# One-hot gate products placed one token at a time inside the second expert pass of a two-block transformer kernel

## The chip, the cores and the metric

The kernel runs on one core of one Trainium2 chip. The metric is the device time of one execution in microseconds (us); lower is better.

## The reference, cut to what matters

Two transformer blocks follow each other on 256 tokens of width 1024. The change lies in the last part of the second block, a feed-forward layer that picks 128 of 16,384 experts for each token:

```python
# PEER_HEADS 8, PEER_TOPK 16, PEER_NKEYS 128: e = i1 * 128 + i2, for each token 8 * 16 picks
e = (i1 * PEER_NKEYS + i2).reshape(TOK_BLOCK, PEER_HEADS * K)
gate = jax.nn.softmax(best_s, axis=-1).reshape(TOK_BLOCK, PEER_HEADS * K)
u = expert_u[e]
act = jax.nn.gelu(jnp.einsum('td,ted->te', xb, u), approximate=False)
coef = (gate * act.astype(jnp.float32)).astype(xb.dtype)
return jnp.einsum('te,ted->td', coef, expert_v[e])
```

## The kernel before, in words

The kernel gathers nothing: it computes all 16,384 experts, as 128 tiles of 128 (a tile `e` holds the experts of one second key with all 128 first keys), and zeroes what was not picked. Each weight tile is 128 x 1024 in fp32 and passes through three buffers (`ring`, RING = 3). Since a matmul in fp32r keeps only the high part of a number, ScalarE copies each tile to `w_hi` (`split_high`, L474), and VectorE (two tiles of three) or GpSimd (the third) forms `w_lo` = tile - `w_hi` (`split_low`, L488). The DMA of a tile (L528) waits until the tile three before it was split.

**First expert pass.** TensorE multiplies the tiles of `expert_u` with the tokens (`expert_up`, L673) and ScalarE puts gelu of it into `act_all`, 128 experts x (128 tiles x 256 tokens). **Second expert pass.** For each tile of `expert_v` (`expert_down`, L1130) TensorE adds coefficient times weights into the PSUM banks 4 to 7, which hold 256 tokens x 1024 outputs: 12 matmuls with 512 columns, six for each half of the tokens (three products high x high, high x low, low x high, two column halves each). The coefficients of tile e are split just ahead: ScalarE writes `h_hi` (`high_coef`, L2045) and VectorE `h_lo` (`low_coef`, L1709), into two sets of buffers (e % 2).

**Gates.** The mask with the softmax weights is made by matmuls with one-hot operands, for 64 tiles (half of the second keys) at a time. For four tokens (a "quad" q) VectorE writes the one-hot rows of the first key (`first_keys(q)`, L1656, 128 x 512, three buffers in turn, semaphore `hot_1_ready`). For eight tokens (a group g = q // 2) it writes those of the second key (`second_keys(g)`, L1667), and GpSimd multiplies them by the softmax weights (`weigh(g)`, L625, `hot_2_ready`). TensorE forms one 128 x 64 product for each token into a bank of its own (`four_gates(q)`, L1095, banks 0 to 2 in turn, fp32), and VectorE multiplies the bank into `act_all` (`gated_acts(g)`, L1677, `gates_used`). Quads 0 to 63 serve the first half of the tiles, quads 64 to 127 the second half, which the second pass needs only from tile 64 on. So quads 68 to 127 are computed during the second pass.

**The order of work around the change** is written out by hand for each engine, and each engine executes its list in order. In the loop of 60 steps (tiles k = 2 to 61):

- TensorE: `expert_down(k)`, which waits for `w_lo` of tile k and for `coef_low` k + 1, then `four_gates(66 + k)`.
- VectorE, step k (`down_dve`, L1720): `low_coef(k + 2)`, which waits for ScalarE's `high_coef(k + 2)`; `split_low` of tile k + 3, where it is not GpSimd's; `first_keys(67 + k)`; then `gated_acts(33 + k // 2)` for odd k, `second_keys(34 + k // 2)` for even k.
- ScalarE, step k: `high_coef(k + 2)`, which waits until TensorE has signalled the end of tile k, since that frees the `h` buffers; then `split_high` of tile k + 3.
- GpSimd, step k: `split_low` of every third tile, and for even k `weigh(34 + k // 2)`.

Two lists side by side, of the same step:

```python
# VectorE                                  # TensorE
second(k, i, GB)                           expert_down(k, i, GB)
if k < 61:                                 four_gates(66 + k, i)
    first_keys(67 + k, i)
```

Of the kernel before, what the change touches and what calls it, by code (L numbers as in the profile page):

```python
# [122 lines left out]
def bass_transformer_pair(nc, x_t, meta_t, kept, first, second, rel, w1_in, w1_cmp, w1_out, w1_ffn,  # L123
# [3 lines left out]
    with ExitStack() as ctx:  # L127
# [3 lines left out]
        def sem(name):  # L131
            return ctx.enter_context(nc.semaphore(name))
# [15 lines left out]
        psum = ctx.enter_context(nc.psum_tensor("psum", [P, 8, 512], F32))  # L148
# [75 lines left out]
        coef_low = sem("coef_low")  # L224
        tiles_used = sem("tiles_used")
# [121 lines left out]
        GB = 12  # L347
# [10 lines left out]
        hot_2 = lambda g: hot_2_sets[g % 2]  # L358
        hot_1_read = lambda q: hot_1(q) if q % 3 == 0 else hot_1(q).bitcast(F32)
        gate_bank = lambda g: 6 + g % 2 if g < GROUPS else g % 3  # L360
# [76 lines left out]
        hot_1_ready = sem("hot_1_ready")  # L437
        hot_2_raw = sem("hot_2_raw")
        hot_2_ready = sem("hot_2_ready")
        gates_done = sem("gates_done")  # L440
        gates_used = sem("gates_used")
# [14 lines left out]
        base, n = [], 0  # L456
# [6 lines left out]
        def trip(v, i=None, per=BODY):  # L463

            return v if i is None else i * per + v
# [10 lines left out]
        def low_wait(eng, n, i=None, per=BODY):  # L476

            if n % RING == 2:
                eng.wait_ge(low_ready2, trip(n // RING + 1, i, per // RING))
            else:  # L480
                eng.wait_ge(low_ready, trip(n // RING * 2 + n % RING + 1, i, per // RING * 2))
# [9 lines left out]
        def tile_split(pe, n, i=None, per=BODY):  # L491

            low_wait(pe, n, i, per)
            return n % RING
# [3 lines left out]
        B_V = B_EXP + NE  # L498
# [158 lines left out]
        def _(pe):  # L657
# [25 lines left out]
            def down(slot, par):  # L683

                for m in range(KD):
                    for w, h in ((w_hi, h_hi), (w_hi, h_lo), (w_lo, h_hi)):
# [9 lines left out]
                      start=True, stop=True).then_inc(brow_sum, 1)  # L696
# [3 lines left out]
            with pe.Fori(0, Z1 // BODY) as i:  # L700
                for k in range(BODY):
                    slot = tile_split(pe, B_IN1 + k, i)
# [4 lines left out]
            for qt in range(2):  # L707
                for k in range(KD):
                    mm = pe.matmul(psum[:, 6, qt * 24:(qt + 1) * 24], sq[:, k, qt * P:(qt + 1) * P],
                                   colv("gates", k * 24, (k + 1) * 24), start=(k == 0), stop=(k == KD - 1))  # L710
# [4 lines left out]
            for kv in range(2):  # L715
                for j in range(4):
                    slot = tile_split(pe, B_CMP + kv * 4 + j)
                    for r in range(4):
                        for n, (w, x) in enumerate(((w_hi, x_hi), (w_hi, x_lo), (w_lo, x_hi))):
                            mm = pe.matmul(psum[0:2 * N_CMP, kv, 0:2 * P], x[:, 4 * kv + j, r * 2 * N_CMP:(r + 1) * 2 * N_CMP],  # L720
                                           w[:, slot, 2 * r * P:2 * (r + 1) * P],
                                           start=(j + r + n == 0), stop=(j + r + n == 8))
                    mm.then_inc(tiles_used, 1)

            for b, zt in enumerate((ZVS, ZVW)):
                for kt in range(2):
                    mm = pe.transpose(psum[:, 4, (b * 2 + kt) * P:(b * 2 + kt + 1) * P],
                                      z1[:, zt, kt * P:(kt + 1) * P], const("ident"))
            mm.then_inc(vtok_sum, 1)
            pe.wait_ge(cmp_hid_ready, 2)  # L730
            for kv in range(2):
                for c in range(2):
                    mm = pe.transpose(psum[:, 2, (2 * kv + c) * 32:(2 * kv + c) * 32 + 2 * N_CMP],
                                      cmp_act[0:2 * N_CMP, kv, c * P:(c + 1) * P], const("ident")[0:2 * N_CMP, 0:2 * N_CMP])
            mm.then_inc(cmp_hid_sum, 1)
            pe.wait_ge(cmp_hid_ready, 3)
            for c in range(2):
                pe.matmul(psum[:, 5, 0:2 * N_CMP], colv("w2k", c * P, (c + 1) * P), cmp_hid[:, 0, c, :],
                          start=(c == 0), stop=(c == 1))
            for g in range(N_KV):  # L740
                for c in range(2):
                    mm = pe.matmul(psum[0:N_CMP, 5, 64 + g * HD:64 + (g + 1) * HD],
                                   cmp_hid[:, 1, c, g * N_CMP:(g + 1) * N_CMP], colv("w2v", c * HD, (c + 1) * HD),
                                   start=(c == 0), stop=(c == 1))
# [7 lines left out]
            for n in range(6):  # L752
                pe.matmul(psum[:, BIAS_BANKS[n], :], const("flip"), bias_up.rearrange("p h k -> p (h k)")[:, n * 512:(n + 1) * 512],
                          start=True, stop=True).then_inc(bias_turned, 1)
# [66 lines left out]
            for m in range(KD):  # L821
                slot = tile_split(pe, B_OUT1 + m)
# [63 lines left out]
            for n, (lo, hi, w, src) in enumerate(((0, HD, "wa_up", 20), (HD, P, "wa_up", 20), (0, P, "g_up", 21))):  # L886
                pe.wait_ge(lowrank_ready, 2)
                for m in range(4):
                    if n == 2:
                        pe.wait_ge(up_ready, m + 1)  # L890
                    mm = pe.matmul(psum[:, (4 * n + m) % 8, 0:T2], colv(w, m * P, (m + 1) * P)[lo:hi], z2[lo:hi, src, 1:T2 + 1],
                                   start=True, stop=True)
                    mm.then_inc(up_sum, 1)

            for r, (ready, src) in enumerate(((kk_squares, sq4), (bonus_in, sq4))):
# [3 lines left out]
                for m in range(4):  # L899
                    mm = pe.matmul(psum[:, 4 + m, 0:T2], const("headones"), src[:, m, :], start=True, stop=True)  # L900
# [6 lines left out]
            def fm(x, h, t0, nt):  # L907

                q = slice(h % 2 * HD, (h % 2 + 1) * HD)
                return x[q, h // 2, t0:t0 + nt]  # L910

            for tg in range(3):
# [3 lines left out]
                for n, src in enumerate((alpha, z2[:, 16:20, 1:T2 + 1], kappa_end, beta_end)):  # L916
                    if tg == 0 and n == 2:
                        pe.wait_ge(kappa_ready, 1)
                    for m in range(4):
                        mm = pe.transpose(psum[0:nt, n, m * P:(m + 1) * P], src[:, m, t0:t0 + nt], const("ident"))  # L920
                    mm.then_inc(tm_sum, 1)
                for hh in range(2):
# [14 lines left out]
                    for n, kinds in enumerate((((beta, alpha), (kappa, alpha)), ((alpha, beta),), ((beta, rho), (kappa, rho)))):  # L937
                        for odd in range(2):
                            for k, (x, y) in enumerate(kinds):
                                for h in (odd, odd + 2):  # L940
                                    mm = pe.matmul(out(2 * n + odd, 2 * k + h // 2), fm(x, 4 * hh + h, t0, nt),
                                                   fm(y, 4 * hh + h, t0, nt), start=True, stop=True)
# [38 lines left out]
                    for h in range(4):  # L981
                        q = slice(h % 2 * HD, (h % 2 + 1) * HD)
# [3 lines left out]
                        mm = pe.matmul(psum[q, 5, c:c + nt], yh(h, HD, P), G(G_QT, h), start=False, stop=True)  # L986
                    mm.then_inc(eo_sum, 1)
                    if tg < 2:
                        for p in range(2):
                            n = 2 * u + p  # L990
                            pe.wait_ge(spread_b, 3 * u + 2 + p)
                            pe.wait_ge(spread_y, 3 * u + 1 + 2 * p)
                            for x in range(2):
                                h = 2 * p + x
                                q = slice(x * HD, (x + 1) * HD)
# [5 lines left out]
                                mm = pe.matmul(psum[q, b0 + 1, :], tmh(3, h), ex(2), start=False, stop=True)  # L1001
# [6 lines left out]
                for c in range(nt // CH):  # L1008
                    slot = 8 if tg and c == 0 else c
                    pe.wait_ge(state_ready, 8 * tg + c + 1)  # L1010
                    if tg < 2:
                        for h in range(8):
                            q = slice(h % 2 * HD, (h % 2 + 1) * HD)
                            mm = pe.matmul(psum[q, c % 2, h // 2 * HD:(h // 2 + 1) * HD], f_t[q, h // 2, c, :],
                                           state[q, h // 2, slot, :], start=True, stop=True)
                        mm.then_inc(rec_sum, 1)
                    for h in range(8):
                        q = slice(h % 2 * HD, (h % 2 + 1) * HD)
                        mm = pe.matmul(psum[q, 2, h // 2 * P + c * CH:h // 2 * P + (c + 1) * CH], state[q, h // 2, slot, :],
                                       e_t[q, h // 2, c * CH:(c + 1) * CH], start=True, stop=True)  # L1020
# [24 lines left out]
            for m in range(KD):  # L1045
                if m >= 4:
                    pe.wait_ge(merged_ready, m - 3)
                slot = tile_split(pe, B_MID + 16 + m)
# [3 lines left out]
            for m in range(KD):  # L1052
                slot = tile_split(pe, B_OUT2 + m)
# [4 lines left out]
            for m in range(16):  # L1058
                slot = tile_split(pe, B_Q + m)
# [3 lines left out]
            for n in range(2):  # L1063
                slot = tile_split(pe, B_SUB + n)
                if n == 0:
                    pe.wait_ge(q_copied, 16)
                for qt in range(2):
                    if n == 1:
                        pe.wait_ge(score_copied, 2 * qt + 2)
                    for k in range(8):  # L1070
                        for p, w in enumerate((w_hi, w_lo)):
                            mm = pe.matmul(psum[:, 4 * qt + k // 4 + 0, (k % 4) * P:(k % 4 + 1) * P],
                                           query[:, 8 * n + k, qt * P:(qt + 1) * P], w[:, slot, k * P:(k + 1) * P].bitcast(F32),
                                           start=(p == 0), stop=(p == 1))
# [6 lines left out]
            def expert_up(e, i=None, per=BODY):  # L1081
                slot = tile_split(pe, B_EXP + e, i, per)
                pe.wait_ge(expert_act, trip(e + 1, i, per))
                project(slot, psum[:, e % BODY, 0:TX], TX).then_inc(tiles_used, 1)

            def four_gates(q, i=None):

                g = q // 2
                pe.wait_ge(hot_1_ready, trip(q + 1, i, GB))
                if q % 2 == 0:  # L1090
                    pe.wait_ge(hot_2_ready, trip(g + 1, i, GB // 2))
                    pe.wait_ge(gates_used, trip(g + 1, i, GB // 2))
                bank = psum[:, gate_bank(g), :].rearrange("p (e t) -> p t e", t=8)
                for t in range(4):
                    mm = pe.matmul(bank[:, 4 * (q % 2) + t, :], hot_1_read(q)[:, t, :], hot_2(g)[:, 4 * (q % 2) + t, :],  # L1095
                                   start=True, stop=True)
                mm.then_inc(gates_done, 1)

            pieces(B_EXP, E0 - 1, pe, expert_up)

# [2 lines left out]
            for n in range(3):  # L1103
                for qt in range(2):
                    mm = pe.transpose(psum[:, 6 + n // 2, (n % 2) * TX + qt * P:(n % 2) * TX + (qt + 1) * P],
                                      chosen[:, n, qt].rearrange("p a b -> p (a b)"), const("ident"))
# [9 lines left out]
            for q in range(60, 64):  # L1116
                four_gates(q)
# [6 lines left out]
                    pe.matmul(psum[:, 4 + 2 * tt + k // 4, (k % 4) * P:(k % 4 + 1) * P], hx1[:, k, tt * P:(tt + 1) * P],  # L1124
                              const("ident"), start=(k % 4 == 0), stop=False, is_transpose=True, skip_group_check=True)

            def half_down(slot, par, tt):
                for w, h in ((w_hi, h_hi), (w_lo, h_hi), (w_hi, h_lo)):
                    for half in range(2):
                        mm = pe.matmul(psum[:, 4 + 2 * tt + half, :], h[:, par, tt * P:(tt + 1) * P],  # L1130
                                       w[:, slot, half * 512:(half + 1) * 512], start=False, stop=False,
                                       skip_group_check=True)
                return mm

            def expert_down(e, i=None, per=BODY):
                slot = tile_split(pe, B_V + e, i, per)
                pe.wait_ge(coef_low, trip(e + 1, i, per))
                half_down(slot, e % 2, 0)
                half_down(slot, e % 2, 1).then_inc(tiles_used, 1)

            expert_down(0)
            expert_down(1)
            for q in range(64, 68):
                four_gates(q)
            with pe.Fori(0, 5) as i:
                for k in range(2, 2 + GB):
                    expert_down(k, i, GB)
                    four_gates(66 + k, i)
            pieces(B_V, NE - 2 - 62, pe, lambda k, i: expert_down(62 + k, i))
            expert_down(NE - 2)  # L1150
            slot = tile_split(pe, B_V + NE - 1)
# [1009 lines left out]
```

## Time and profile before

| what | value |
|---|---|
| median of 3 runs (lowest, highest) | 1799.74 us (1796.98, 1811.25) |
| profiled execution, its own time | 1801.02 us |
| profiled execution, span of its trace | 1799.2 us |
| TensorE matmuls busy | 1625.5 us, 90% of the span |
| VectorE busy | 1123.3 us, 62% |
| ScalarE busy | 773.6 us, 43% |
| GpSimd busy | 473.7 us, 26% |
| mean granted clock of TensorE | 0.949 of full speed |

The profile is one execution. Its span runs from the first to the last instruction; what lies around it is 1.8 us. Engines are named PE (TensorE matmuls), PEld (its weight loads), DVE (VectorE), ACT (ScalarE), POOL (GpSimd), SP (the engine that issues the DMAs). Matmuls are pipelined and their ends are modelled, so a busy PE is not PE at its peak. A row with x2 joins two instructions, and its duration is from the start of the first to the end of the last.

### The profile page before, as it was taken

How to read it: one execution, taken by the hardware profiler on the slowest of the kernel's cores; microseconds unless marked ns; L12 is line 12 of the kernel's file. 1: busy time of each engine (PE TensorE's matmuls, PEld its weight loads, DVE VectorE, ACT ScalarE, POOL GpSimd, SP SyncE). 2: the span in 40 equal slices, each digit the busy share in tenths (PEclk: the TensorE clock that was granted, in tenths of full speed). 3: DMA queues.
4: the chain of work that ended last, by engine and by line, in shares of the span. 5: the costliest groups of instructions: out<-in, count | busy, mean ns of one | idle time of the engine just before them, and what ended most of it. 6: DMA issues, size and time to landing. Idle time of an engine off the chain costs nothing.

```text
span 1799.2 us, 32624 instructions
## 1 busy us (share of the span) xinstructions
PE 1625.5 (90%) x11880; PEld 1478.1 (82%) x11880; DVE 1123.3 (62%) x1793; ACT 773.6 (43%) x1203; POOL 473.7 (26%) x235
## 2 busy tenths in 40 slices
PE   6988789997994777788899999999999999999998
PEld 5965689996993665578899999999998888888886
DVE  3366366565358566675428898656667777775554
ACT  3455455554443111124446566544332333335554
POOL 1210112221231221012222323433333333332322
PEclk8997899999997899789999999999998999999999
DMA  6540235553451000014445555544442444446654
GB/s 217 187 133 1 94 106 185 186 176 117 131 167 54 1 2 1 2 60 151 133 150 177 172 187 175 164 141 146 144 140 94 141 139 135 136 139 198 187 196 154
DMA packets 66240, 234.70 MB, mean 130 GB/s; under 512 B 8216, under 2 KB 9256, under 8 KB 66176
## 3 DMA queue, kind: packets, MB, share of 16 engines
q1 hardware_dynamic: 65776, 232.25, 39.8%
q0 software_dynamic: 400, 1.59, 0.2%
q8 instruction: 42, 0.69, 0.2%
q14 instruction: 22, 0.18, 0.0%
HBM read 232.74 MB, written 1.06 MB: 130 GB/s over the span
## 4 chain that ended last, share of the span: by engine, by line
PE 57%; issue 30%; DVE 7%; POOL 3%; ACT 2%; DMA 0%; SPq 0%; POOLq 0%; DVEq 0%; ACTq 0%
PE psum L673 25%; PE psum L1130 18%; PE psum L1095 6%; PE psum L687 3%; POOL w_lo L488 3%; PE psum L949 2%; DVE big L1387 1%; DVE w_lo L488 1%; DVE big L1401 1%; ACT w_hi L474 1%; PE psum L661 1%; DVE big L1428 0%; DMA big<-rel 0%; DVE x_hi L1656 0%; DVE big L1456 0%
## 5 line engine op out<-in xcount | busy, mean ns | idle before, releaser
L673 PE MATMUL psum<-x_hi,w_hi 128*128 128x256 f32 (+1 forms) x2192 | 628.9, 287 | 44.3 <-DVE x_lo L1193 23.3
L673 PE MATMUL psum<-x_lo,w_hi 128*128 128x256 f32 (+1 forms) x2192 | 623.4, 284 | 0.0
L673 PE MATMUL psum<-x_hi,w_lo 128*128 128x256 f32 (+1 forms) x2192 | 623.0, 284 | 0.0
L488 POOL TENSOR_TENSOR w_lo<-ring,w_hi 128x1024 fp32r<-128x1024 f32 x144 | 363.7, 2526 | 939.9 <-ACT w_hi L474 939.9
L488 DVE TENSOR_TENSOR w_lo<-ring,w_hi 128x1024 fp32r<-128x1024 f32 x290 | 366.1, 1263 | 247.1 <-ACT w_hi L474 246.4
L474 ACT ACTIVATE w_hi<-ring 128x1024 fp32r<-128x1024 f32 x434 | 456.1, 1051 | 86.0 <-PE psum L673 47.7
L673 PEld LDWEIGHTS psum<-x_hi,w_hi 128*128 128x128 f32 x2192 | 420.4, 192 | 50.5 <-issue 31.3
L673 PEld LDWEIGHTS psum<-x_hi,w_lo 128*128 128x128 f32 x2192 | 420.4, 192 | 0.0
L673 PEld LDWEIGHTS psum<-x_lo,w_hi 128*128 128x128 f32 x2192 | 418.4, 191 | 0.0
L1130 PE MATMUL psum<-w_hi,h_hi 128*128 128x512 f32 x512 | 164.4, 402 | 0.0
L2045 ACT ACTIVATE h_hi<-big 128x256 fp32r (+1 forms) x128 | 53.3, 417 | 250.6 <-PE psum L1130 243.1
L1130 PE MATMUL psum<-w_lo,h_hi 128*128 128x512 f32 x512 | 159.3, 393 | 0.0
L1130 PE MATMUL psum<-w_hi,h_lo 128*128 128x512 f32 x512 | 158.2, 390 | 0.0
L1709 DVE TENSOR_TENSOR h_lo<-big,h_hi 128x256 fp32r<-128x256 f32 x128 | 75.3, 589 | 117.9 <-ACT h_hi L2045 117.5
L2018 ACT ACTIVATE big<-psum 128x256 f32 (+1 forms) x128 | 49.0, 383 | 201.1 <-PE psum L673 200.9
L1130 PEld LDWEIGHTS psum<-w_hi,h_lo 128*128 128x128 f32 x512 | 96.4, 188 | 21.4
L1130 PEld LDWEIGHTS psum<-w_lo,h_hi 128*128 128x128 f32 x512 | 96.4, 188 | 21.1
L1130 PEld LDWEIGHTS psum<-w_hi,h_hi 128*128 128x128 f32 x512 | 92.0, 190 | 15.5
L1327 DVE SCALAR_TENSOR_TENSOR big<-psum,big 128x255 f32<-128x255 f32 x88 | 42.4, 482 | 71.0 <-ACT big L1868 69.5
L949 PE MATMUL psum<-big 128*128 128x128 f32 (+4 forms) x480 | 64.3, 299 | 19.4 <-DVE big L1456 7.7
L949 PEld LDWEIGHTS psum<-big 128*128 128x128 f32 (+1 forms) x480 | 55.5, 183 | 27.5 <-DVE big L1456 8.7
L625 POOL TENSOR_TENSOR kept_sb<-kept_sb,sq 128x512 f32<-128x512 f32 x32 | 35.9, 1122 | 108.1 <-DVE kept_sb L1667 108.1
(297 smaller groups left out, 2004.2 us busy)
## 6 DMA issues: line engine op xcount, KB each, us to landing
ring<-experts SPq DMA_DIRECT2D x256, 512.0 KB, 3.3
ring<-w_ffn SPq DMA_DIRECT2D x66, 512.0 KB, 3.4
ring<-w_in SPq DMA_DIRECT2D x46, 512.0 KB, 3.6
ring<-w_mid SPq DMA_DIRECT2D x24, 512.0 KB, 3.3
ring<-w_out SPq DMA_DIRECT2D x16, 512.0 KB, 4.0
ring<-w_q SPq DMA_DIRECT2D x16, 512.0 KB, 3.6
ring<-w_cmp SPq DMA_DIRECT2D x8, 512.0 KB, 3.3
big<-bias_rows POOLq DMA_DIRECT2D x1, 1536.0 KB, 8.6
```

Of the source, the lines that this page charges most:

```text
L474: act.activation(w_hi[:, n % RING, :], ring[:, n % RING, :], ACT.Copy).then_inc(high_ready, 1)
L488: eng.tensor_tensor(w_lo[:, n % RING, :], ring[:, n % RING, :], w_hi[:, n % RING, :].bitcast(F32), ALU.subtract).then_inc(low_ready2 if n ...
L625: pool.tensor_tensor(hot_2(g), hot_2(g), chosen_t[:, 0, bass.ds(at, 8)].unsqueeze(2).to_broadcast([P, 8, HALF]), ALU.mult).then_inc(hot_2_ ...
L673: mm = pe.matmul(dst, w[:, slot, k * P:(k + 1) * P], x[:, k, t0:t0 + width], start=(n == 0), stop=(n == 3 * len(chunks) - 1))
L687: mm = pe.matmul(psum[:, 4 + m // 2, (m % 2) * TX:(m % 2 + 1) * TX], w[:, slot, m * P:(m + 1) * P], h[:, par, :], start=False, stop=False, ...
L949: mm = pe.matmul(dst, G(a, h), r, start=True, stop=True)
L1095: mm = pe.matmul(bank[:, 4 * (q % 2) + t, :], hot_1_read(q)[:, t, :], hot_2(g)[:, 4 * (q % 2) + t, :], start=True, stop=True)
L1130: mm = pe.matmul(psum[:, 4 + 2 * tt + half, :], h[:, par, tt * P:(tt + 1) * P], w[:, slot, half * 512:(half + 1) * 512], start=False, stop ...
L1327: ins = dve.scalar_tensor_tensor(out=c[:, back:TX], in0=psum[:, 2 * par + half, 0:TX - back], scalar=taps[:, par, 3 * half + 2 - back:3 * ...
L1709: dve.tensor_tensor(h_lo[:, e % 2, :], act_all[:, trip(e, i, per), :], h_hi[:, e % 2, :].bitcast(F32), ALU.subtract).then_inc(coef_low, 1)
L2018: act.activation(act_all[:, trip(e, i), :], psum[:, e % BODY, 0:TX], ACT.Gelu).then_inc(expert_act, 1)
L2045: act.activation(h_hi[:, e % 2, :], act_all[:, trip(e, i), :], ACT.Copy).then_inc(coef_high, 1)
```

## The change

`four_gates` is cut into `one_gate(q, t)`, which issues the product of one token; its waits (`hot_1_ready`, and for even q also `hot_2_ready` and `gates_used`) stand ahead of t = 0, and the signal `gates_done` behind t = 3. In the loop of 60 steps `half_down` calls it behind the second and the fourth of its six matmuls. So the four products of quad 66 + k stand behind matmuls 2, 4, 8 and 10 of the 12 of tile k, where before all four stood behind the twelfth. Elsewhere `four_gates` stays. No list of another engine is changed.

```diff
+            def one_gate(q, t, i=None):
+
+                g = q // 2
+                if t == 0:
+                    pe.wait_ge(hot_1_ready, trip(q + 1, i, GB))
+                    if q % 2 == 0:
+                        pe.wait_ge(hot_2_ready, trip(g + 1, i, GB // 2))
+                        pe.wait_ge(gates_used, trip(g + 1, i, GB // 2))
+                bank = psum[:, gate_bank(g), :].rearrange("p (e t) -> p t e", t=8)
+                mm = pe.matmul(bank[:, 4 * (q % 2) + t, :], hot_1_read(q)[:, t, :], hot_2(g)[:, 4 * (q % 2) + t, :],
+                               start=True, stop=True)
+                if t == 3:
+                    mm.then_inc(gates_done, 1)
+
             def four_gates(q, i=None):
...
                 for t in range(4):
...
+                    one_gate(q, t, i)
...
-            def half_down(slot, par, tt):
+            def half_down(slot, par, tt, between=None):
+                n = 0
                 for w, h in ((w_hi, h_hi), (w_lo, h_hi), (w_hi, h_lo)):
                     for half in range(2):
                         mm = pe.matmul(psum[:, 4 + 2 * tt + half, :], h[:, par, tt * P:(tt + 1) * P],
                                        w[:, slot, half * 512:(half + 1) * 512], start=False, stop=False,
                                        skip_group_check=True)
+                        n += 1
+                        if between is not None and n in (2, 4):
+                            between(2 * tt + n // 2 - 1)
                 return mm
...
+            def expert_down_gates(e, q, i):
+                slot = tile_split(pe, B_V + e, i, GB)
+                pe.wait_ge(coef_low, trip(e + 1, i, GB))
+                one = lambda t: one_gate(q, t, i)
+                half_down(slot, e % 2, 0, one)
+                half_down(slot, e % 2, 1, one).then_inc(tiles_used, 1)
...
             with pe.Fori(0, 5) as i:
                 for k in range(2, 2 + GB):
-                    expert_down(k, i, GB)
-                    four_gates(66 + k, i)
+                    expert_down_gates(k, 66 + k, i)
```

## Rows read from the trace of the kernel before

**Rows 1.** The page: granted clock of TensorE in 40 slices of the span

```profile
PEclk8997899999997899789999999999998999999999
```

**Rows 2.** The chain that ended last, in order of time: start, us, what

```profile
1383.95 2.82 PE psum L1130 x12
...
1611.87 178.26 PE psum L1130 x786
```

**Rows 3.** Busy time by stretch: us, PE, PEld, DVE, ACT, POOL, PEclk, DMA share, GB/s

```profile
1384.00:1612.00 228.00, 224.22 (x1202) 186.65 (x1202) 176.25 (x220) 81.57 (x120) 82.13 (x50) 1.00 0.42 137
```

**Rows 4.** Waits in 1384:1612: who waited for whom, us, times, longest

```profile
ACT h_hi L2045 <- PE psum L1130: 148.5, 60, 5.0
```

**Rows 5.** Groups of instructions in 1384:1612, by form

```profile
L488 DVE TENSOR_TENSOR w_lo<-ring,w_hi 128x1024 fp32r<-128x1024 f32 x40 | 50.8, 1271 | 11.2 <-ACT w_hi L474 11.2
```

**Rows 6.** Timeline of PE around three gate blocks: start, us, what

```profile
1461.71 0.61 PE L1130 MATMUL psum<-w_hi,h_lo 128*128 128x512 f32 x2
1462.61 1.07 PE L1095 MATMUL psum<-kept_sb,x_hi 128*128 128x64 f32 x8 [0.29 <-DVE x_hi L1656]
...
1464.04 0.63 PE L1130 MATMUL psum<-w_lo,h_hi 128*128 128x512 f32 x2
1464.51 0.62 PE L1130 MATMUL psum<-w_hi,h_lo 128*128 128x512 f32 x2
...
1466.35 1.00 PE L1095 MATMUL psum<-kept_sb,x_lo 128*128 128x64 f32 x8
1467.16 0.71 PE L1130 MATMUL psum<-w_hi,h_hi 128*128 128x512 f32 x2
1467.70 0.63 PE L1130 MATMUL psum<-w_lo,h_hi 128*128 128x512 f32 x2
...
1473.67 1.02 PE L1095 MATMUL psum<-sq,x_hi 128*128 128x64 f32 x8
```

**Rows 7.** Timeline of ACT behind the tile that ends at 1462.32

```profile
1462.46 0.42 ACT L2045 ACTIVATE h_hi<-big 128x256 fp32r x1 [2.29 <-PE psum L1130]
1462.79 1.04 ACT L474 ACTIVATE w_hi<-ring 128x1024 fp32r<-128x1024 f32 x1
```

**Rows 8.** Timeline of DVE in the same stretch, and one later first_keys

```profile
1461.70 0.68 DVE L1656 TENSOR_TENSOR x_hi<-kept_sb,sq 128x512 fp32r<-128x512 f32 x1
...
1463.02 0.42 DVE L1709 TENSOR_TENSOR h_lo<-big,h_hi 128x256 fp32r<-128x256 f32 x1
1463.86 1.22 DVE L488 TENSOR_TENSOR w_lo<-ring,w_hi 128x1024 fp32r<-128x1024 f32 x1 [0.41 <-ACT w_hi L474]
1465.00 0.68 DVE L1656 TENSOR_TENSOR x_lo<-kept_sb,sq 128x512 fp32r<-128x512 f32 x1
...
1472.85 0.68 DVE L1656 TENSOR_TENSOR x_hi<-kept_sb,sq 128x512 fp32r<-128x512 f32 x1
```

**Rows 9.** Timeline of all engines where GpSimd splits the tile, no L488 on DVE

```profile
1431.22 0.61 PE L1130 MATMUL psum<-w_hi,h_lo 128*128 128x512 f32 x2
...
1431.97 0.42 ACT L2045 ACTIVATE h_hi<-big 128x256 fp32r x1 [2.32 <-PE psum L1130]
...
1432.87 0.69 DVE L1656 TENSOR_TENSOR sq<-kept_sb,sq 128x512 f32<-128x512 f32 x1
```

**Rows 10.** Timeline of PE behind three idle gaps in earlier stages

```profile
237.53 0.36 PE L673 MATMUL psum<-x_hi,w_hi 128*128 128x256 f32 x1 [3.38 <-DVEq L1310]
...
795.92 0.55 PE L673 MATMUL psum<-x_hi,w_hi 128*128 128x256 f32 x1 [2.34 <-POOL w_lo L488]
...
799.24 0.28 PE L673 MATMUL psum<-x_hi,w_hi 128*128 128x256 f32 x1
...
801.95 0.36 PE L673 MATMUL psum<-x_hi,w_hi 128*128 128x256 f32 x1 [1.50 <-DVE w_lo L488]
```

**Rows 11.** Busy time by stretch behind the first two of these gaps, columns as in rows 3

```profile
237.00:239.00 2.00, 1.47 (x12) 1.50 (x13) 2.00 (x4) 0.36 (x1) 0.00 (x0) 1.00 0.01 4
797.00:799.00 2.00, 2.00 (x11) 2.00 (x11) 2.00 (x1) 0.00 (x0) 0.00 (x0) 0.50 0.70 246
```

More of the change, by code:

```diff
@@ L1084, in expert_up @@
                 project(slot, psum[:, e % BODY, 0:TX], TX).then_inc(tiles_used, 1)
-            def four_gates(q, i=None):
[L1088 to L1093, printed above, removed]
+            def one_gate(q, t, i=None):
[10 more added lines that the diff above has]
+                    mm.then_inc(gates_done, 1)
+            def four_gates(q, i=None):
                 for t in range(4):
-                    mm = pe.matmul(bank[:, 4 * (q % 2) + t, :], hot_1_read(q)[:, t, :], hot_2(g)[:, 4 * (q % 2) + t, :],
-                                   start=True, stop=True)
-                mm.then_inc(gates_done, 1)
+                    one_gate(q, t, i)
             pieces(B_EXP, E0 - 1, pe, expert_up)
```

## The prediction

> **What bounds the kernel now.** I read the busy shares and clock slices, the chain of waits, then the stretch of the changed loop, then single tiles in the timeline. TensorE is the bound, at a clock of nine tenths or more in the last 20 slices but one [rows 1]. In the changed loop, from 1383.95 to 1611.87 us on the chain [rows 2], it is busy 224.22 of 228 us, always at 1.00 [rows 3]: 227.9 us for 60 tiles, 3.80 us each. The other engines have slack as shares (VectorE 176.25 of 228 us), but a share doesn't say when they are done. The waits do: ScalarE waits for TensorE's tile end before each of the 60 `h_hi` writes, 148.5 us in all [rows 4]. So a chain starts at the end of each tile, and it matters what TensorE wants from its end.
>
> One tile shows it. It ends on TensorE at 1461.71 + 0.61 = 1462.32 [rows 6]. ScalarE then writes `h_hi` at 1462.46 and `w_hi` from 1462.79 to 1463.83 [rows 7]; VectorE writes `h_lo` at 1463.02, `w_lo` at 1463.86, and only then `first_keys`, 1465.00 to 1465.68 [rows 8]. That is 3.36 us behind the tile's end. TensorE meanwhile did the gate block, a whole further tile, and asks for these keys at the next block, at 1466.35 [rows 6]: 0.67 us to spare. Other blocks have none: the block at 1462.61 waited for keys that ended at 1462.38, and that at 1473.67 for keys that ended at 1473.53 [rows 6, 8]. The keys come just in time for a place behind the tile. This is what the change touches.
>
> **The change part by part.** Nothing is removed or added in work: the same 12 wide matmuls and four products (eight instructions on TensorE, since each is made in two passes), the same three waits. No DMA moves in its queue. What moves is the wait for `first_keys(66 + k)`: from behind matmul 12 of tile k to behind matmul 2.
>
> *The wait.* `first_keys(66 + k)` stands in VectorE's step k - 1, behind `low_coef(k + 1)`. That waits for `high_coef(k + 1)`, which waits for the end of tile k - 1. VectorE can't run ahead of it however idle it is. Count from E, the modelled end of tile k - 1. Two matmuls of tile k start behind it and end about E + 0.45 (spacing 0.23, modelled duration 0.39). The keys end at E + 3.36 where VectorE splits the tile (again 1472.85 + 0.68 = 1473.53 against an end at 1470.16), and at E + 1.73 where GpSimd does (1431.22 + 0.61 = 1431.83; keys 1432.87 + 0.69 = 1433.56 [rows 9]). From keys to the first product it takes 0.14 us for odd q (1473.53 to 1473.67) and 0.23 for even q with its three waits (1462.38 to 1462.61) [rows 6, 8], 0.19 in the mean. So the first product starts at E + 3.55 in 40 tiles and E + 1.92 in 20; the split between the two is the count of VectorE's `w_lo`, x40 of 60 [rows 5]. Behind the waiting product stand ten wide matmuls, three products and the signal that frees `h` and the ring, and ScalarE, VectorE and GpSimd wait for that signal. So the delay isn't absorbed: each tile starts the next chain only at its own late end.
>
> *The rest of a tile.* Behind the first product's start: ten wide matmuls, nine spacings of 0.232 us (half of 1464.04 to 1464.51 is 0.235, other pairs 0.23 [rows 6]) and the last one's 0.38 = 2.47 us; four products at (1467.16 - 1466.35) / 4 = 0.20 us = 0.81 us; and a switch. The first pair of wide matmuls behind products takes 0.54 us (1467.16 to 1467.70 [rows 6]) against 0.46, so 0.08 us per return. Before there is one return in a tile, now four: 0.32 us. Sum 3.60 us.
>
> Tiles take 3.55 + 3.60 = 7.15 us (40 of them) and 1.92 + 3.60 = 5.52 us (20): 286 + 110.4 = 396.4 us against 227.9. That is +168.5 us at full clock. The cost of interleaving itself isn't in the trace of before. From below: products among wide matmuls might cost less than in a block, since their weight loads lie under a wide matmul; at half price they give back 4 x 0.10 x 60 = 24 us, and without the extra returns another 14. From above: I take twice the return cost, +19 us. I keep 0.20 and 0.08, the nearest rows.
>
> The Trainium skill ("TensorE: Matmul & The Clock Gate", section Part 2: What happens when you issue a matmul) says that weight loads are pulled ahead of running matmuls, which argues for spreading the products. By that rule the sum would be some 24 us smaller. The same section says the matmuls themselves stay in program order, so nothing behind the waiting product can pass it.
>
> *GpSimd and VectorE.* `second_keys`, `weigh` and `gated_acts` are late only if a step is shorter than their work. They come behind `first_keys` in a step that is now longer, so they fall into TensorE's ten matmuls. I take them at nothing; if that cover fails, one more 0.68 us operation of VectorE a tile would be on the chain, 41 us.
>
> *The clock.* TensorE will now idle some 3.55 - 0.45 = 3.1 us in 40 tiles and 1.5 us in 20. Earlier stages show such gaps: behind 1.50 us the next matmul spacing stayed that of full clock; behind 2.34 us of idle the granted clock stood at 0.50 (1.2 GHz), and the matmuls ran so from 795.92 to 799.24, 3.32 us, which loses half of it, 1.6 us; behind 3.38 us of idle it stood at 1.00 [rows 10, 11]. A gap of 3.1 lies between one that fell and one that didn't. I take a fall at 24 of the 40: 24 x 1.6 = 37 us. The ends are no fall (0) and, as an estimate, a fall at every one that lasts half as long again, over the two matmuls of the next tile too (40 x 2.5 = 100).
>
> The skill (same page, section Why this matters for your kernels) warns that idle gaps between bursts of matmuls send the clock back to half; the gap of 2.34 us agrees, that of 3.38 us doesn't.
>
> Sum: 1801.0 + 168.5 + 37 = 2006 us for the profiled execution. The median of the runs shown is 1.3 us lower: 2005 us.
>
> **The rivals.** (1) *Full clock holds.* The stall comes as worked out, and the clock doesn't fall, as behind the 3.38 us gap: 1968 us, down to 1930 with cheap products and no extra returns. Against it: the gap of 2.34 us. (2) *The clock falls and stays down.* The 3.6 us of work in every tile take twice as long, 60 x 3.6 = 216 us more: about 2184 us, and any mixture down to 2075. Against it: behind 795.92 it came back while TensorE was dense for 3.3 us, about the length of a tile's work. (3) *The keys are there in time* and the kernel gets faster. The place that decides is the second matmul of a tile: keys would have to end before E + 0.3. Then 60 groups of products at half price and the short waits of before (228 - 224.22 = 3.8 us idle) give -24 - 4: 1772 us. For it: VectorE has 52 us of slack in the stage. Against it: the order of VectorE's list, in which these keys stand behind `low_coef(k + 1)`, and rows 8 and 9, in which they never end earlier than E + 1.7. (4) *A smaller stall*, because VectorE's operations overlap more than in the rows: 1850 to 1930 us.
>
> **How the numbers follow.** Forecast (stall, clock falling in part of the gaps) 0.60; rival 1 0.20; rival 2 0.12; rival 3 0.02; rival 4 0.06. The time given is 2005 us. The range 1945 to 2075 holds the forecast, whose own range is 1978 to 2068 (1968 and 10 to 100 for the clock), and most of rival 1. A measurement of this kernel tells about 1% from no change. Faster by over 1% 0.02, within 1% 0.01, slower 0.97.
>
> **What would show it.** In the profile after: the loop is 400 to 450 us instead of 228; "PE psum L1095" (by its new line) waits for `first_keys`, some 40 times about 3.1 us and 20 times about 1.5, where before the longest wait was 0.3; tiles of two lengths in a pattern of three; clock slices below 9 in this stage only; the 64 tiles behind the loop still at 2.72 us each (178.26 / 786 x 12 [rows 2]). I'm wrong if the waits for keys stay under 1 us, or if the loop's time without idle grows by more than the switches and the clock account for.

## The result, and the profile after

The changed kernel takes 2027.65 us (median of 4 runs, 2020.6 to 2032.57) against 1802.97 us for the kernel before, measured beside it: a ratio of 1.125, 95% interval 1.122 to 1.129. That is 225 us more, where 205 were forecast. The time lies in the forecast range (1945 to 2075), and the direction and the mechanism were those forecast. Two terms were off in opposite directions: the waits were put some 11 us too high and the clock 26 us too low.

The page of the kernel after, engine slices and granted clock. The changed loop lies in slices 28 to 36 of 40:

```profile
span 2023.9 us, 32624 instructions
...
PE   6987899979947778889999999997666766769998
...
PEclk9977999999969887999999999998888888889999
```

The slices of TensorE fall from 9 to 6 and 7 there, and the clock to 8. Behind the loop both come back.

Busy time by stretch: the loop, and the 64 tiles behind it (columns as in [rows 3], to which the first answers):

```profile
1386.00:1836.00 450.00, 304.59 (x1225) 240.60 (x1224) 165.86 (x222) 81.25 (x119) 79.96 (x50) 0.84 0.22 71
1836.00:2015.00 179.00, 179.00 (x791) 148.22 (x791) 90.41 (x109) 88.15 (x130) 50.44 (x21) 1.00 0.57 182
```

450 us instead of 228 for nearly the same instructions. TensorE is now idle for 145 us, and the other engines, which have the same work to do in twice the time, are idle for longer too. Where [rows 3] showed TensorE as the bound, here no engine is: that is what a chain of waits looks like in shares.

Who waited for whom, 1386 to 1836 us (us in total, times, longest; L1672 is `first_keys`, L2061 `high_coef`, L1137 the wide matmuls):

```profile
ACT h_hi L2061 <- PE psum L1137: 364.0, 59, 9.5
DVE h_lo L1725 <- ACT h_hi L2061: 264.1, 59, 6.7
...
PE psum L1095 <- DVE x_hi L1672: 60.7, 20, 3.2
PE psum L1095 <- DVE x_lo L1672: 58.3, 20, 3.1
PE psum L1095 <- DVE sq L1672: 26.3, 20, 1.5
```

All 60 products that come first in a tile wait for `first_keys`: 40 times some 3.0 us, 20 times 1.3 us. The sum is 145 us, the whole idle time of TensorE. The first line answers to [rows 4]: ScalarE's wait for the tile's end grew from 148.5 to 364.0 us. TensorE waits for VectorE, which waits for ScalarE, which waits for TensorE.

One tile behind a split on GpSimd and one behind a split on VectorE, on TensorE (start, us, what; answers to [rows 6]):

```profile
1508.90 0.41 PE L1095 MATMUL psum<-kept_sb,sq 128*128 128x64 f32 x2 [1.30 <-DVE sq L1672]
1509.12 0.70 PE L1137 MATMUL psum<-w_lo,h_hi 128*128 128x512 f32 x2
1509.66 0.33 PE L1095 MATMUL psum<-kept_sb,sq 128*128 128x64 f32 x2
1509.80 0.71 PE L1137 MATMUL psum<-w_hi,h_lo 128*128 128x512 f32 x2
1510.35 0.63 PE L1137 MATMUL psum<-w_hi,h_hi 128*128 128x512 f32 x2
...
1511.64 0.71 PE L1137 MATMUL psum<-w_hi,h_lo 128*128 128x512 f32 x2
1512.18 0.62 PE L1137 MATMUL psum<-w_hi,h_hi 128*128 128x512 f32 x2
1515.76 0.43 PE L1095 MATMUL psum<-kept_sb,x_hi 128*128 128x64 f32 x2 [2.95 <-DVE x_hi L1672]
...
1518.15 1.20 PE L1137 MATMUL psum<-w_lo,h_hi 128*128 128x512 f32 x2
```

The gap of 2.95 us stands behind the first two wide matmuls of the tile (1512.18), before its first product. A pair of wide matmuls takes 0.71 us at full clock (1511.64) and 1.20 behind the long gap (1518.15): the clock fell within the tile. The granted clock there (columns as in [rows 3], the clock third from the end):

```profile
1518.00:1520.00 2.00, 2.00 (x9) 1.71 (x7) 0.00 (x0) 0.00 (x0) 0.00 (x0) 0.50 0.01 4
```

The other side of that gap, on VectorE (answers to [rows 8]):

```profile
1513.04 0.42 DVE L1725 TENSOR_TENSOR h_lo<-big,h_hi 128x256 fp32r<-128x256 f32 x1 [3.78 <-ACT h_hi L2061]
1513.88 1.22 DVE L488 TENSOR_TENSOR w_lo<-ring,w_hi 128x1024 fp32r<-128x1024 f32 x1 [0.41 <-ACT w_hi L474]
1515.02 0.68 DVE L1672 TENSOR_TENSOR x_hi<-kept_sb,sq 128x512 fp32r<-128x512 f32 x1
```

The tile ended at 1511.64 + 0.71 = 1512.35. The keys end at 1515.70, 3.35 us later; [rows 8] gave 3.36. VectorE idled 3.78 us before this chain; its list puts the keys behind it. No run here moves them ahead of the coefficients.

From one `h_hi` write to the next, tiles behind GpSimd's splits take 5.30 us (20 of them), and those behind VectorE's 8.57 us (mean of 39 behind the loop's first). Two of these 39 took 6.8 and 6.9 us: there the clock stayed. Five took 9.8 to 9.9 us: there it stayed low for twice as long as in the others.

### The profile page after: what moved, and what is told of

Read it like the earlier page. It is cut to its first block, busy times and chain, and to the rows that moved or that the text cites. A ratio compares the mean times of both kernels' runs of the same rounds, so it can differ in the third digit from the quotient of the medians.

```text
span 2023.9 us, 32624 instructions
## 1 busy us (share of the span) xinstructions
PE 1709.2 (84%) x11880; PEld 1531.6 (76%) x11880; DVE 1110.7 (55%) x1793; ACT 773.3 (38%) x1203; POOL 470.7 (23%) x235
## 4 chain that ended last, share of the span: by engine, by line
PE 54%; issue 29%; DVE 9%; ACT 4%; POOL 3%; DVEq 0%; DMA 0%; ACTq 0%; SPq 0%; POOLq 0%
PE psum L673 22%; PE psum L1137 19%; PE psum L1095 6%; PE psum L687 3%; POOL w_lo L488 3%; ACT w_hi L474 2%; PE psum L949 2%; DVE w_lo L488 1%; DVE big L1403 1%; DVE sq L1672 1%; DVE x_lo L1672 1%; DVE x_hi L1672 1%; ACT h_hi L2061 1%; DVE big L1417 0%; PE psum L661 0%
## 5 line engine op out<-in xcount | busy, mean ns | idle before, releaser
L488 POOL TENSOR_TENSOR w_lo<-ring,w_hi 128x1024 fp32r<-128x1024 f32 x144 | 362.2, 2515 | 1084.7 <-ACT w_hi L474 1084.7
L488 DVE TENSOR_TENSOR w_lo<-ring,w_hi 128x1024 fp32r<-128x1024 f32 x290 | 363.3, 1254 | 253.2 <-ACT w_hi L474 252.5
L1725 DVE TENSOR_TENSOR h_lo<-big,h_hi 128x256 fp32r<-128x256 f32 x128 | 64.5, 505 | 344.3 <-ACT h_hi L2061 344.2
L2061 ACT ACTIVATE h_hi<-big 128x256 fp32r (+1 forms) x128 | 53.3, 417 | 470.8 <-PE psum L1137 461.2
L1137 PE MATMUL psum<-w_lo,h_hi 128*128 128x512 f32 x512 | 190.2, 456 | 0.0
L1137 PE MATMUL psum<-w_hi,h_lo 128*128 128x512 f32 x512 | 190.2, 456 | 0.0
L1137 PE MATMUL psum<-w_hi,h_hi 128*128 128x512 f32 x512 | 175.3, 427 | 0.0
L1137 PEld LDWEIGHTS psum<-w_hi,h_hi 128*128 128x128 f32 x512 | 108.5, 212 | 25.5
L1137 PEld LDWEIGHTS psum<-w_lo,h_hi 128*128 128x128 f32 x512 | 98.2, 214 | 10.7
L1137 PEld LDWEIGHTS psum<-w_hi,h_lo 128*128 128x128 f32 x512 | 98.2, 214 | 10.7
L625 POOL TENSOR_TENSOR kept_sb<-kept_sb,sq 128x512 f32<-128x512 f32 x32 | 34.9, 1089 | 148.5 <-DVE kept_sb L1683 148.5
```

What stands on the lines that cost most here:

```text
L488: eng.tensor_tensor(w_lo[:, n % RING, :], ring[:, n % RING, :], w_hi[:, n % RING, :].bitcast(F32), ALU.subtract).then_inc(low_ready2 if n ...
L1725: dve.tensor_tensor(h_lo[:, e % 2, :], act_all[:, trip(e, i, per), :], h_hi[:, e % 2, :].bitcast(F32), ALU.subtract).then_inc(coef_low, 1)
L2061: act.activation(h_hi[:, e % 2, :], act_all[:, trip(e, i), :], ACT.Copy).then_inc(coef_high, 1)
```

## The experiments

The theory: `first_keys` can't begin before a tile's end, so a wait for it early in the next tile stops TensorE until it is done, in all 60 tiles, and in the long gaps the clock falls. The rivals: mixing narrow matmuls (the products, 64 columns) and wide ones (512 columns) is itself slow; or the slow matmuls have another cause than the gaps.

**The wait alone, moved.** The three waits stay where the change put them; the products go back into a block behind the tile.

```diff
+                def wait_alone(t):
+                    g = q // 2
+                    if t == 0:
+                        pe.wait_ge(hot_1_ready, trip(q + 1, i, GB))
...
-                half_down(slot, e % 2, 0, one)
-                half_down(slot, e % 2, 1, one).then_inc(tiles_used, 1)
...
+                half_down(slot, e % 2, 0, wait_alone)
+                half_down(slot, e % 2, 1).then_inc(tiles_used, 1)
+                for t in range(4):
+                    one_gate(q, t, i, wait=False)
```

> The three waits stand behind matmul 2 as in the changed kernel, the four products stay in one block behind the tile's signal, as before. Theory (the early wait for first_keys is the cause): the signal no longer has products ahead of it, so a tile takes 3.36 + 0.19 + 2.47 = 6.0 us where VectorE splits and 1.73 + 0.19 + 2.47 = 4.4 us where GpSimd does; 40 and 20 of them are 328 us against 228, 1903 us at full clock, up to 1965 us if the clock still falls in gaps of some 2.2 us. Rival (mixing narrow and wide matmuls is the cause): with the products back in a block the time is that of before, about 1803 us.

Measured: 1938.65 us, ratio 1.076 (1.070 to 1.082). Without one product between wide matmuls, 137 us of the 225 remain. The difference is where the theory puts it: the signal for ScalarE no longer stands behind products, and where the clock holds tiles take 4.2 to 4.5 and 6.0 to 6.2 us (forecast 4.4 and 6.0). The clock fell in 22 of the 60 tiles, behind gaps of 1.8 to 2.3 us. The first rival, as the main cause, falls.

**The products later in the tile.**

```diff
-                        if between is not None and n in (2, 4):
-                            between(2 * tt + n // 2 - 1)
+                        if between is not None and n in (3, 4, 5, 6):
+                            between(n - 3)
...
-                half_down(slot, e % 2, 0, one)
+                half_down(slot, e % 2, 0)
```

> Products interleaved as in the changed kernel, but behind matmuls 9, 10, 11 and 12 of a tile. Theory: the wait comes 1.6 us later in the tile, so where GpSimd splits nothing is waited for (3.7 us a tile), and where VectorE splits the tile takes 3.5 + 1.6 = 5.1 us with a gap of about 1.1 us, too short for the clock to fall: loop 277 us, total about 1852 us, clock 1.00 in the loop. Rival (mixing narrow and wide matmuls is the cause): as many switches as in the changed kernel, so about 2028 us.

Measured: 1855.63 us, ratio 1.030 (1.022 to 1.038). The same number of switches between narrow and wide costs 54 us here and 225 before. The wait comes seven matmuls later, and with it the products; the fourth now stands behind the signal for ScalarE. Where GpSimd splits, tiles take 3.65 us with no wait, as forecast; where VectorE splits, 5.0 to 5.2 us in most tiles, with gaps of 1.1 to 1.3 us. In ten tiles the gap was 1.6 to 1.7 us and the tile took 5.5 us or more; in five of these the clock fell, which was not expected.

**The keys ahead of the split on VectorE**, in the changed kernel.

```diff
             def down_dve(k, i=None):
-                second(k, i, GB)
+                low_coef(k + 2, i, GB)
                 if k < 61:
                     first_keys(67 + k, i)
+                split_low(dve, B_V + k + 3, i, per=GB)
```

> The changed kernel, with first_keys ahead of split_low in VectorE's step, nothing else. Theory: the keys then end 1.7 us behind the tile's end in every tile, all 60 take the 5.3 us of the tiles that GpSimd splits, gaps are 1.3 us and the clock stays at 1.00: loop 318 us, total about 1894 us. Rival (w_lo or the second keys hold TensorE, or the clock falls for another reason than the long gaps): 1980 us or more.

Measured: 1894.52 us, ratio 1.051 (1.043 to 1.060), where about 1894 was expected; the two executions lie 8.6 us apart, so that close a match is luck. The loop took 323.5 us, 318 expected. The kernel does the same work on every engine as the changed one; swapping two operations of VectorE takes back 133 us. Busy time by stretch in its loop:

```profile
1400.00:1690.00 290.00, 214.66 (x1097) 168.33 (x1098) 148.12 (x201) 73.62 (x108) 72.52 (x46) 1.00 0.29 98
```

Behind 59 of the 60 gaps, of 1.1 to 1.5 us, the clock stayed at 1.00. It fell once, in the loop's first tile, which follows a block of 16 products:

```profile
1383.02 0.41 PE L1095 MATMUL psum<-kept_sb,x_lo 128*128 128x64 f32 x2 [1.54 <-DVE x_lo L1672]
1383.23 1.12 PE L1137 MATMUL psum<-w_lo,h_hi 128*128 128x512 f32 x2
```

**More work in the gap.** Six, then twelve more wide matmuls, into a bank that nothing reads, between the tile's second matmul and the wait; the twelve only in the 40 tiles that follow a split on VectorE.

```diff
+                        if filler and n == 2:
+                            for _ in range(filler):
+                                pe.matmul(psum[:, 3, :], h[:, par, tt * P:(tt + 1) * P], w[:, slot, 0:512],
+                                          start=True, stop=True, skip_group_check=True)
                         if between is not None and n in (2, 4):
...
-                half_down(slot, e % 2, 0, one)
+                half_down(slot, e % 2, 0, one, filler=6)
```

> The changed kernel, with six more 512-column matmuls into an unused PSUM bank behind matmul 2, ahead of the wait: 1.4 us more work on TensorE in each of 60 tiles. Theory (the long gap lets the clock fall, which costs 1.6 us in each of 38 tiles): the gap shrinks from 3.0 to 1.6 us, the clock holds, and the kernel gets faster though it does more: about 1965 us. Rival (the matmuls behind the wait are slow for another reason): 2028 us or, with the work in the way, up to 2110 us.

Measured: 1986.18 us, ratio 1.102 (1.096 to 1.109). Faster than the changed kernel by 41 us though it does more, so the direction is the theory's; but the clock held in fewer tiles than expected: 15 of 39 tiles behind VectorE's splits still took 8.5 to 8.7 us, the others 6.8 to 7.1. It fell behind 14 of the 19 gaps of about 1.8 us and behind 1 of the 19 of about 1.6 us. Hence the next run, which closes the gap.

> The changed kernel with twelve more 512-column matmuls into an unused bank ahead of the wait, only in the 40 tiles that follow a split on VectorE: 2.8 us more work in each, all inside the gap of 3.0 us. Theory (the gap's length and nothing else lowers the clock): gaps of 0.2 to 0.4 us, no fall, these tiles take 6.97 us as at full clock, the others 5.3; loop 385 us, total about 1803 + 157 = 1960 us, less than the 1986 us of the run with six. Rival (part of the slow matmuls has another cause): 1985 us or more.

Measured: 1960.16 us, ratio 1.085 (1.077 to 1.093), as expected. Busy time by stretch in the loop, six and then twelve:

```profile
1400.00:1700.00 300.00, 249.02 (x1132) 197.74 (x1131) 121.52 (x162) 60.19 (x88) 56.40 (x37) 0.93 0.23 77
```

```profile
1400.00:1700.00 300.00, 268.05 (x1309) 213.28 (x1308) 128.59 (x172) 64.22 (x94) 61.92 (x39) 1.00 0.23 81
```

With twelve the clock is 1.00 and every tile behind a split on VectorE takes 6.8 to 7.1 us (but the loop's first, 10.0 us with the block of 16 products ahead of it). The changed kernel's own tile without a fall took 6.9 us. So this loop is that of the changed kernel at full clock: from the `h_hi` write behind tile 1 to that behind tile 61 it takes 387.8 us (1378.90 to 1766.69), the changed kernel 451.2 (1385.44 to 1836.64), the kernel before 230.5 (1380.57 to 1611.07). The waits, with what the other places of the products change, cost 157 us and the clock 63 us.

**What interleaving is worth without the waits.** Three runs: the kernel before with the keys ahead of the split (the diff above); the changed kernel with each tile taking the products of one quad earlier; and both.

```diff
-            for q in range(64, 68):
+            for q in range(64, 67):
                 four_gates(q)
...
-                    expert_down_gates(k, 66 + k, i)
-            pieces(B_V, NE - 2 - 62, pe, lambda k, i: expert_down(62 + k, i))
+                    expert_down_gates(k, 65 + k, i)
+            expert_down(62)
+            four_gates(127)
+            pieces(B_V, NE - 2 - 63, pe, lambda k, i: expert_down(63 + k, i))
```

> The kernel before (products in a block), with first_keys ahead of split_low on VectorE. If the keys' lateness costs the kernel before its short waits (3.80 us a tile against 2.78 + 0.89 = 3.67 us of work), the loop takes 220 us instead of 228: about 0.4% faster, 1795 us against 1803. If those waits have another cause: no difference.

> The changed kernel's places, but in tile k the products of quad 65 + k instead of 66 + k: its keys were begun one tile earlier, 0.3 us ahead of the place by the rows. Theory (only the lead of the keys matters, interleaving is free): between 1791 and 1803 us, the clock at 1.00. Rival (interleaving itself costs): over 1810 us. Rival (interleaving saves TensorE time by hidden weight loads): under 1785 us.

> Both: quad 65 + k in tile k, and first_keys ahead of split_low. No wait is left in the loop, so it takes what TensorE's work takes: 60 x 3.66 = 220 us if a product interleaved costs what it does in a block (0.22 us with the return to wide matmuls), about 1795 us and equal to the run with the block and early keys. If hidden weight loads made it cheaper it would be below that run; if the switches cost, above it.

| kernel | median | ratio to before (95%) | loop in the trace |
|---|---|---|---|
| before, keys first | 1790.81 us | 0.9946 (0.9924 to 0.9968) | 222.2 us |
| quad later | 1798.18 us | 0.9978 (0.9961 to 0.9995) | 227.3 us |
| quad later, keys first | 1797.45 us | 0.9964 (0.9942 to 0.9985) | 222.6 us |

The loops of the first and the third (1376.48 to 1598.65 and 1384.91 to 1607.49) are equal within 0.4 us of 222: no tile waits in either, and behind the first nearly all take 3.66 or 3.67 us. Interleaving neither costs nor saves there. The 6.6 us between the medians don't come from the loop: in the profiles the third enters it 8.4 us later, lost before 221 us, in the attention of the first block, where the granted clock from 140 to 221 us is 0.88 in the first kernel and 0.78 in the third. Nor do they belong to the kernels: each has executions near 1790 us (1788 to 1791, mean clock 0.949 to 0.951) and near 1797 us (1797 to 1798, 0.940 to 0.948), six and two of 8 in the first, three and nine of 12 in the third.

The timelines show why it is even. A block in the first kernel, and products inside the tile in the third:

```profile
1452.06 1.00 PE L1095 MATMUL psum<-sq 128*128 128x64 f32 x8
1452.87 0.71 PE L1130 MATMUL psum<-w_hi,h_hi 128*128 128x512 f32 x2
1453.41 0.63 PE L1130 MATMUL psum<-w_lo,h_hi 128*128 128x512 f32 x2
1453.88 0.62 PE L1130 MATMUL psum<-w_hi,h_lo 128*128 128x512 f32 x2
```

```profile
1455.59 0.33 PE L1095 MATMUL psum<-kept_sb,x_hi 128*128 128x64 f32 x2
1455.73 0.71 PE L1137 MATMUL psum<-w_lo,h_hi 128*128 128x512 f32 x2
...
1456.28 0.33 PE L1095 MATMUL psum<-kept_sb,x_hi 128*128 128x64 f32 x2
```

In the block a product takes (1452.87 - 1452.06) / 4 = 0.20 us, inside the tile 1455.73 - 1455.59 = 0.14 us. But each return to wide matmuls makes the next pair 0.54 or 0.55 us long instead of 0.46 or 0.47 (1452.87 to 1453.41, 1455.73 to 1456.28), once behind a block and four times inside the tile. 4 x 0.20 + 0.08 = 0.88 us against 4 x (0.14 + 0.09) = 0.92 us, equal as far as rows read to 0.01 us can tell.

With the quad taken later alone, most tiles run without a wait, but in four the keys are late after all, by 0.6 to 0.7 us (TensorE, then VectorE and GpSimd, same kernel; L1674 is `first_keys` there):

```profile
1407.34 0.41 PE L1095 MATMUL psum<-kept_sb,sq 128*128 128x64 f32 x2 [0.63 <-DVE sq L1674]
```

```profile
1404.16 2.39 POOL L488 TENSOR_TENSOR w_lo<-ring,w_hi 128x1024 fp32r<-128x1024 f32 x1 [0.18 <-ACT w_hi L474]
1404.18 2.92 DVE L1674 TENSOR_TENSOR sq<-kept_sb,sq 128x512 f32<-128x512 f32 x1
```

An operation that takes 0.68 us elsewhere takes 2.92 us when it begins beside GpSimd's split, and ends 0.55 us behind it. With the keys ahead of the split on VectorE the whole list runs earlier: in the same step of that kernel the keys start at 1403.15 and GpSimd's split at 1403.70, and they take 0.68 us.

## Why the prediction was right, and where its sizes were off

**The wait: right.** The first product was put at 3.55 and 1.92 us behind the tile's end. Measured are 3.51 and 1.85: from the `h_hi` write to the first product 3.37 and 1.71 us in the mean, and 0.14 us from the tile's end to that write. That the delay isn't absorbed, since everything that could catch up waits for the signal behind the waiting product, is shown by the waits of 60 tiles that sum to the idle time of the loop, and by the two runs that move only the wait or only the keys.

**The rest of a tile: 3.60 us forecast, 3.45 measured** (3.59 to the `h_hi` write, less 0.14). The step "four products at 0.20 us and a return at 0.08 each" was off in its first half: a product inside the tile takes 0.14. The saving is taken back by the returns, which no run here explains. The Trainium skill ("TensorE: Matmul & The Clock Gate", Part 2: What happens when you issue a matmul) has weight loads pulled ahead under running matmuls; that a product among wide matmuls is 0.06 us cheaper agrees with it. With both terms the full-clock sum was 168.5 us against the 157 that the run with twelve more matmuls gives.

**The clock: the right mechanism, too small.** The step that failed is "a fall at 24 of the 40" at 1.6 us each (24 x 1.6 is 38, written as 37). In 39 tiles behind a split on VectorE (without the loop's first) the clock fell in 37, and the loop's first took 10.9 us against 10.0 in the run with twelve more matmuls. The cost of one fall was nearly right: 63 us over these 38 tiles is 1.7 us in the mean, with five of them at about twice that. I had placed 3.1 us between two single gaps of earlier stages and took a share in the middle, a guess and not a reading. The gap of 3.38 us at which the clock held was the exception; why it held there was not tried. In the changed kernel gaps of 2.8 to 3.2 us sent the clock to 0.50, at 1.2 GHz, in 37 of 39 tiles. The Trainium skill's warning (same page, Why this matters for your kernels) that idle gaps between bursts of matmuls do so now agrees with the trace. Sum: 157.3 + 63.4 = 220.7 us in the loop. The traces differ by 2023.9 - 1799.2 = 224.7: 4.9 us more were lost ahead of the loop (1385.44 against 1380.57), and 0.9 us was gained behind it, where the kernel before still makes its last block of products.

That the sum came within 20 us is in part luck: the waits were 11 us too dear and the clock 26 us too cheap.

**The rivals.** Full clock (1968 us) was 0.20 and is what the run with filled gaps shows at 1960. A clock that stays down fell: in the tiles that follow a split on GpSimd, from the first product's start to the `h_hi` write it took 3.5 to 3.6 us, full clock. Keys in time fell; with the list of VectorE as it stands they can't be. Of the signs named ahead, the waits (3.0 and 1.3 us, forecast 3.1 and 1.5), the pattern of three and the 64 tiles behind the loop (2.72 us each) came; a loop of 400 to 450 us was 451. "Clock slices below 9 in this stage only" was no sign: earlier stages have such slices too, as they had before the change [rows 1].

**The small finding in the kernel before**, that its keys come just in time, was right too: moved ahead of the split they save 8.3 us in the loop (230.5 to 222.2) and 0.5% in all. That kernel has the lowest median of this study; the interleaved one with the quad later and the keys first has an equal loop, and no interleaved one is faster.

## What to carry to other kernels

Before moving work earlier on one engine, write down for each wait that moves with it when its producer can start. If the producer waits for the end of the unit of work just before, nothing placed at the head of the next unit can use it, whatever the busy shares say; swap the producer's own operations first, here for 0.5% at no work. A wait put into the middle of an in-order list also holds the signal at the list's end, so a stall repeats in every step and isn't absorbed. And where the stall is long enough to lower TensorE's clock, price that as well: it was 28% of the loss here.

## What the runs showed that I had not expected

- More work made the kernel faster: six more wide matmuls in each of 60 tiles took 41 us off the changed kernel, twelve in 40 tiles 67 us.
- The clock fell behind gaps far shorter than 3 us: 14 of 19 of about 1.8 us (the run with six), five of ten of 1.6 to 1.7 us (products later), one of 60 of 1.1 to 1.5 us (keys first), against 37 of 39 of 2.8 to 3.2 us. The gap's length alone doesn't decide: in the run with the wait alone most gaps behind VectorE's splits were 2.0 to 2.3 us, and the clock fell in 22 of 60 tiles.
- A VectorE operation of 0.68 us took 2.92 us beside GpSimd's `tensor_tensor`; `second_keys`, too, took 2.88 us eight times in the kernel before with the keys first, at no cost to TensorE, which doesn't wait in that loop.
